# A decoder block on one core: the last output columns in two strided parts, gate rows by wide products, the state coefficients folded into C

## The reference, cut to what matters

```
mod = silu(c) @ w_ada + b_ada                      # six vectors of 1024: sh1 sc1 gt1 sh2 sc2 gt2
h = rms_norm(x, g_mix) * (1 + sc1) + sh1
u, q, k, v, ga, gb = split(h @ w_in)
# branch A: complex diagonal state space, 32 groups of 16 channels, 64 states each
bbar = coef * b                                    # coef, b complex, coef per (group, state)
state[t] = abar * state[t-1] + bbar @ u[t]
y = Re(c_re + i c_im applied to state) + d * u
y_a = glu(gelu(y) @ w_glu)
y_b = attention(rotary(q), rotary(k), v) @ w_attn_o
x = x + gt1 * ((sigmoid(ga) * y_a + sigmoid(gb) * y_b) @ w_out)
h2 = rms_norm(x, g_ffn) * (1 + sc2) + sh2
x = x + gt2 * experts(h2)                          # router, top 4 of 32, each expert:
        # gate_up = h2 @ w_gu[e] (1024 by 2048), clamped SwiGLU, @ w_down[e] (1024 by 1024)
out = rms_norm(x, g_final)
```

## Time and profile before

| what | value |
| --- | --- |
| median of three runs | 1161.6 us (1161.04 to 1162.45) |
| the profiled execution's own time | 1159.92 us |
| its span | 1158.0 us |
| TensorE busy | 1122.6 us (97%) |
| VectorE busy | 442.8 us (38%) |
| ScalarE busy | 140.9 us (12%) |
| GpSimd busy | 105.1 us (9%) |
| moved by DMA | 459.46 MB, mean 397 GB/s |
| chain that ended last | TensorE 78%, DMA 18% |

### The profile page before, as it was taken

How to read it: one execution, slowest core, us unless ns; L and a number is a source line. 1 busy time by engine, 2 the same in 40 slices (tenths; PEclk the granted TensorE clock), 3 DMA queues, 4 the chain that set the end, 5 groups by cost and what they waited for, 6 DMA issues and landing times.

```text
span 1158.0 us, 17087 instructions
## 1 busy us (share of the span) xinstructions
PE 1122.6 (97%) x6970; PEld 491.0 (42%) x6970; DVE 442.8 (38%) x952; ACT 140.9 (12%) x313; POOL 105.1 (9%) x142
## 2 busy tenths in 40 slices
PE   8999999999999999999999999999999999999996
PEld 6657788544333333333333333333333333333332
DVE  7857668263222333332222322222222222222224
ACT  3222240231000000000000000000000000000002
POOL 6496810000000000000000000000000000000000
PEclk9999999999999999999999999999999999999999
DMA  9983389999999999999999999999999999999994
GB/s 385 393 305 102 101 335 400 421 349 422 423 427 434 428 428 430 431 430 430 430 434 429 429 432 430 431 425 431 431 430 431 430 431 432 431 431 426 427 424 202
DMA packets 39839, 459.46 MB, mean 397 GB/s; under 512 B 3732, under 2 KB 4248, under 8 KB 16120
## 3 DMA queue, kind: packets, MB, share of 16 engines
q1 hardware_dynamic: 39088, 458.09, 94.3%
q10 hardware_dynamic: 712, 0.81, 0.2%
HBM read 457.83 MB, written 1.05 MB: 396 GB/s over the span
## 4 chain that ended last, share of the span: by engine, by line
PE 78%; DMA 18%; DVE 1%; ACT 1%; issue 1%; SPq 1%; DVEq 0%
PE ps L1086 30%; PE ps L1133 17%; DMA ring<-in_w_gu 16%; PE ps L662 5%; PE ps L1054 4%; PE ps L998 3%; PE ps L847 2%; PE ps L659 2%; PE ps L1110 2%; PE ps L865 2%; DMA ring<-in_first 1%; PE ps L830 1%; PE ps L922 1%; PE ps L623 1%; PE ps L629 1%; PE ps L1118 1%
## 5 line engine op out<-in xcount | busy, mean ns | idle before, releaser
L1086 PE MATMUL ps<-ring,zone 128*64 128x512 f32 x1024 | 227.0, 595 | 9.6 <-DMA ring<-in_w_gu 9.6
L1133 PE MATMUL ps<-ring,tmp 128*64 128x512 f32 x1012 | 224.2, 594 | 10.4 <-ACT tmp L1363 10.4
L1086 PE MATMUL ps<-zone 128*64 128x512 f32 x1024 | 227.2, 595 | 1.3 <-DMA zone<-in_w_gu 1.2
L1854 DVE TENSOR_TENSOR x_tok<-x_tok,ps 128x512 f32<-128x512 f32 x128 | 81.9, 681 | 261.4 <-PE ps L1054 260.1
L1086 PEld LDWEIGHTS ps<-ring,zone 128*64 128x64 f32 x1024 | 70.7, 137 | 161.6 <-issue 143.5
L1133 PEld LDWEIGHTS ps<-ring,tmp 128*64 128x64 f32 x1012 | 83.2, 137 | 130.7 <-issue 130.7
L1086 PEld LDWEIGHTS ps<-zone 128*64 128x64 f32 x1024 | 70.7, 137 | 154.1 <-issue 146.9
L1360 ACT ACTIVATE tmp<-hT 128x256 f32<-128x256 f32 x64 | 23.9, 417 | 722.8 <-DVE hT L1869 722.8
L1869 DVE TENSOR_SCALAR hT<-ps 128x256 f32<-128x256 f32 x64 | 24.2, 419 | 189.9 <-PE ps L1086 189.9
L1848 DVE TENSOR_TENSOR tmp<-ps,zone 128x512 f32<-128x512 f32 x32 | 22.1, 691 | 162.8 <-PE ps L1133 162.8
L1054 PE MATMUL ps<-tmp,xn_tok 64*128 64x512 f32 x248 | 70.0, 641 | 0.0
(11 more groups left out here) (339 smaller groups left out, 889.5 us busy)
## 6 DMA issues: line engine op xcount, KB each, us to landing
ring<-in_w_down SPq DMA_DIRECT2D x60, 2048.0 KB, 17.8
zone<-in_w_gu SPq DMA_DIRECT2D x23, 4096.0 KB, 26.9
ring<-in_w_gu SPq DMA_DIRECT2D x23, 4096.0 KB, 29.2
zone<-in_w_gu SPq DMA_DIRECT2D x14, 2048.0 KB, 13.1
ring<-in_w_gu SPq DMA_DIRECT2D x13, 2048.0 KB, 14.1
ring<-in_w_ada SPq DMA_DIRECT2D x16, 1024.0 KB, 13.1
ring<-in_w_in SPq DMA_DIRECT2D x12, 1024.0 KB, 14.6
ring<-in_w_gu SPq DMA_DIRECT2D x10, 1024.0 KB, 9.5
```

The source lines that it names most:

```text
L1086: last = mm(ps[CAP * h:CAP * h + CAP, b, :], hg[:, 2 * j + kk, :], w[:, kk, D * b + 512 * h:D * b + 512 * h + 512], start=False, stop=(j = ...
L1133: last = mm(ps[CAP * h:CAP * h + CAP, 3, :], actT[:, q, j, :], row[:, 512 * h:512 * h + 512], start=False, stop=(j == DN_PIECES - 1 and q ...
L1854: V.tensor_tensor(x_tok[:, t, 512 * h:512 * h + 512], x_tok[:, t, 512 * h:512 * h + 512], ps[:, bank + h, :], ALU.add).then_inc(S["comb_ad ...
```

## The change

1. B comes from the host in block form (`b_layout`, 512 KB in place of 256 KB) and goes straight into `BT`. The six weighting operations of VectorE, ScalarE's spreading, `b_columns` and the copy of its result are gone. In their place VectorE runs `weighted_c` on C: six operations of 512 elements a row, all with both inputs in SBUF, between the signal `phases` and `recurrence(0)`. ScalarE's negation of C (L1264) is gone.
2. `b_u(0)` and `b_u(1)` are one call, pair 1 into banks 6 and 7.
3. `modulation_products` makes two products in place of four, and its transposes have 64 rows. The gates are made directly on all rows by `gate_products` (two products of 512 columns for each n), to which VectorE adds the biases. These come with a new transfer, `gate_laid` (768 KB), behind `xs_read`. `gate_row` and ScalarE's two copies are gone.
4. The last 512 output columns of the second tokens are made in two parts of 256: of each four columns, two. Part 1 goes into bank 7, part 2 into bank 6, which waits for `x1` at 2, since the first half's result lies there. The pieces' `w_used` rises in part 2. Adding, squaring, transposing and routing of the last columns are cut accordingly; one `fill` is gone.

```diff
-    return np.concatenate([b[0].reshape(ST, 2, N, C).transpose(1, 2, 0, 3).reshape(P, ST * C) for b in (b_re, b_im)], axis=1)
+    out = np.zeros((4, 2, C, 2, KW, 2, N), np.float32)
...
+    def by_two(ap):
+        return ap.rearrange("p (n b) -> p n b", b=2)
+    def two_of_four(ap, g):
+        return ap.rearrange("p (n b) -> p n b", b=RUN)[:, :, 2 * g:2 * g + 2]
...
-            sp.dma_start(b_in.rearrange("p r s c -> p (r s c)"), b_laid[:, :]).then_inc(S["const_in"], 16)
+            sp.dma_start(BT.rearrange("p r m n -> p (r m n)"), b_laid[:, :]).then_inc(S["const_in"], 16)
...
             sp.wait_ge(S["xs_read"], KW)
+            sp.dma_start(gates[:, 0:D + W], gate_laid[:, :]).then_inc(S["gates_in"], 16)
             half_gu(0, 1, 0), half_gu(0, 1, 1)
...
             proj(2, 0)
-            b_columns()
             turned_columns(0)
             proj(2, 1, (0,))
-            b_u(0)
+            b_u(0, 1)
             proj(2, 1, (1, 2, 3))
             proj(3, 0)
-            b_u(1)
             turned_columns(1)
...
+                if n == 1:
+                    pe.wait_ge(S["row_sb"], 1)
                 pe.wait_ge(S["ada_used"], KD * n)
                 pe.wait_ge(S["ones_set"], 1)
-                for j in range(4):
-                    last = mm(ps[32 * j:32 * j + 32, MOD_BANK[n], :], ones[:, 0:32], ada_sum[n][:, 512 * j:512 * j + 512],
+                for j in range(2):
+                    own = 512 * (2 * (2 - n) + j)
+                    last = mm(ps[32 * j:32 * j + 32, MOD_BANK[n], :], ones[:, 0:32], ada_sum[n][:, own:own + 512],
...
+            def gate_products(n):
+                pe.wait_ge(S["ada_used"], KD * n)
+                pe.wait_ge(S["ones_set"], 1)
+                for h in range(2):
+                    if n == 1:
+                        last = mm(ps[:, 6 + h, :], ones[:, :], ada_sum[1][:, 512 * h:512 * h + 512], start=True, stop=True, skip_group_check=True)
+                    else:
+                        last = mm(ps[CAP * h:CAP * h + CAP, 7, :], ones[:, 0:CAP], ada_sum[2][:, D + 512 * h:D + 512 * h + 512],
+                                  start=True, stop=True, skip_group_check=True)
                 last.then_inc(S["row_up"], 1)
...
-            for h in range(2):
+            for part, bank in enumerate((6, 7, 6)):
+                if part == 1:
+                    pe.wait_ge(S["row_sb"], 2)
+                if part == 2:
+                    pe.wait_ge(S["x1"], 2)
                 for n in range(4):
...
-                        last = mm(ps[:, 6 + h, :], mergedT[:, k, P:T], w[:, kk, 512 * h:512 * h + 512],
-                                  start=(k == 0), stop=(k == KD - 1))
-                    if h == 1:
+                        if part == 0:
+                            last = mm(ps[:, bank, :], mergedT[:, k, P:T], w[:, kk, 0:W], start=(k == 0), stop=(k == KD - 1))
+                        else:
+                            last = mm(by_two(ps[:, bank, 0:T]), mergedT[:, k, P:T], two_of_four(w[:, kk, W:D], part - 1),
+                                      start=(k == 0), stop=(k == KD - 1))
+                    if part == 2:
                         last.then_inc(w_used, 1)
...
+            def weighted_c():
+                cr, ci = (sprm[:, j, :].unsqueeze(2).to_broadcast([P, ST, 2 * C]) for j in (3, 4))
+                c0, c1 = (CT[:, r].rearrange("p m (s c) -> p (m s) c", s=4) for r in range(2))
+                t0, t1 = (tmp[:, r, :].rearrange("p (s c) -> p s c", s=ST) for r in range(2))
+                link(V.tensor_tensor(t0, c1, ci, ALU.mult))
+                link(V.tensor_tensor(t1, c0, ci, ALU.mult))
+                link(V.tensor_tensor(c0, c0, cr, ALU.mult))
+                link(V.tensor_tensor(c1, c1, cr, ALU.mult))
+                V.tensor_tensor(c0, c0, t0, ALU.subtract).then_inc(S["c_set"], 1)
+                V.scalar_tensor_tensor(c1, t1, -1.0, c1, ALU.mult, ALU.subtract).then_inc(S["c_set"], 1)
+                dve.wait_ge(S["c_set"], 2)
...
             V.engine_nop().then_inc(S["phases"], 1)
+            weighted_c()
...
-            ada_part(8)
+            dve.wait_ge(S["gates_in"], 16)
+            dve.wait_ge(S["row_up"], 1)
+            V.tensor_tensor(gate_mix, ps[:, 6:8, :].rearrange("p b n -> p (b n)"), gate_mix, ALU.add).then_inc(S["row_sb"], 1)
+            ada_part(8), ada_part(9)
             modulation(1)
...
+            def add_two_of_four(g, bank):
+                scr = by_two(xn_tok[:, 1, W + T * g:W + T * g + T])
+                own = two_of_four(x_tok[:, 1, W:D], g)
+                link(V.tensor_tensor(scr, by_two(bank), two_of_four(gate_mix[:, W:D], g), ALU.mult))
+                V.tensor_tensor(own, own, scr, ALU.add).then_inc(S["x1"], 1)
```

More of the change, by code:

```diff
@@ L112, in b_layout, with gate_layout @@
 def b_layout(b_re, b_im):
-    return np.concatenate([b[0].reshape(ST, 2, N, C).transpose(1, 2, 0, 3).reshape(P, ST * C) for b in (b_re, b_im)], axis=1)
+    out = np.zeros((4, 2, C, 2, KW, 2, N), np.float32)
+    for r, w in enumerate((b_re, b_im)):
+        w = w[0].reshape(KW, 4, 2, N, C)
+        for q in range(2):
+            out[:, q, :, r, :, q, :] = w[:, :, q].transpose(1, 3, 0, 2)
+    return out.reshape(P, 2 * KW * P)
+def gate_layout(b_ada):
+    out = np.zeros((P, D + W), np.float32)
+    out[:, 0:D] = b_ada[0, 2 * D:3 * D]
+    for h in range(2):
+        out[CAP * h:CAP * h + CAP, D:] = b_ada[0, 5 * D + W * h:5 * D + W * h + W]
+    return out
 def c_layout(c_re, c_im):
@@ L127, in build @@
 def build(nc, x, w_ada, w_in, w_glu, w_attn_o, w_out, w_router, b_router, w_gu, b_gu, w_down, b_down, g_final,
-          const, head_in, first_in, pair_in, b_laid, c_laid, out):
+          const, head_in, first_in, pair_in, b_laid, c_laid, gate_laid, out):
     ctx = ExitStack()
@@ L665, in proj, with b_u @@
                     last.then_inc(w_used, 1)
-            def b_u(j):
-                if j == 0:
+            def b_u(*pairs):
+                if pairs[0] == 0:
                     pe.wait_ge(S["proj_sb"], 1)
-                    pe.wait_ge(S["BT_sb"], 1)
+                    pe.wait_ge(S["const_in"], 48)
                 else:
-                    pe.wait_ge(S["scanned"], 4 * j)
+                    pe.wait_ge(S["scanned"], 4 * pairs[0])
                 for r in range(2):
[L675 to L680, removed]
+                    for j in pairs:
+                        for q in range(2):
+                            s = 2 * j + q
+                            a = 32 * (s % 4)
+                            last = mm(ps[:, BU_BANK[j] + q, T * r:T * r + T], BT[a:a + 32, r, s // 4, :], uT[a:a + 32, s // 4, :],
+                                      start=True, stop=True, skip_group_check=True)
+                last.then_inc(S["bu_up"], len(pairs))
             def c_x(m):
@@ L806, in modulation_columns @@
                 for cb in range(4):
-                    last = nc.tensor.transpose(ps[:, MOD_BANK[n], P * cb:P * cb + P], modrow.rearrange("p (n b) -> p b n", b=RUN)[:, cb, :], ident)
+                    last = nc.tensor.transpose(ps[:, MOD_BANK[n], CAP * cb:CAP * cb + CAP],
+                                               modrow[0:CAP].rearrange("p (n b) -> p b n", b=RUN)[:, cb, :], ident[0:CAP, 0:CAP])
                 last.then_inc(S["modT_up"], 1)
[L810 to L817, removed]
+            def gate_products(n):
+                pe.wait_ge(S["ada_used"], KD * n)
+                pe.wait_ge(S["ones_set"], 1)
+                for h in range(2):
+                    if n == 1:
+                        last = mm(ps[:, 6 + h, :], ones[:, :], ada_sum[1][:, 512 * h:512 * h + 512], start=True, stop=True, skip_group_check=True)
+                    else:
+                        last = mm(ps[CAP * h:CAP * h + CAP, 7, :], ones[:, 0:CAP], ada_sum[2][:, D + 512 * h:D + 512 * h + 512],
+                                  start=True, stop=True, skip_group_check=True)
                 last.then_inc(S["row_up"], 1)
@@ L915, in _ @@
                     modulation_products(2)
+                    gate_products(2)
                     router_shift()
@@ L1137, in _ @@
             item(0, 0, 1, first=True, odd=32)
-            gate_row(1)
             item_table()
```

114 lines of the change are left out of this document (44 added, 70 removed).

## The result

| | median of the runs | runs |
| --- | --- | --- |
| kernel before | 1160.61 us (1159.24 to 1162.45) | 10 |
| changed kernel | 1164.57 us (1163.61 to 1166.07) | 10 |
| ratio | 1.0036, 95% interval 1.0029 to 1.0044 | |

The change makes the kernel 4.0 us slower. The forecast, 1163.8 us, lies 0.8 us from the measured time and its range holds it. Part of that closeness is luck. The forecast difference was +2.2 us and the measured one is +4.0, so the sum of the steps was too small by 1.8 us. The starting point hid 1.0 us of it: the forecast was laid on the median of three runs, 1161.6 us, and these three belong to the ten above, whose median is 1160.61. By the edge that the prediction set itself, 2.3 us, the change is slower, to which it gave a chance of 0.39; the larger chance, 0.49, went to no change. The experiments have to say which steps were too small.

The account below looks back on a forecast made before the run. DMA bounds the kernel: the end follows the moment it starts running without a gap. Later slots (+0.9) and the later output stage (+1.3) gave +2.2 us, laid on the 1161.6 median: 1163.8 us, range 1159.3 to 1166.8.

Parts of the forecast that it names:

- What bounds the kernel: Whole span: the end is when DMA starts running without a gap, plus 380 MB at 428 GB/s, plus an unchanged tail.
- B's blocks and the joint call: TensorE before turned_columns(1): dropped transposes save 0.9 us, the joint b_u 1.06, making it due at 73.5 instead of 75.47.
- weighted_c meets GpSimd: VectorE before recurrence(0): five of six operations slow to 1.52 us, 8.3 us in all, ending at 66.3 instead of 62.3.
- turned_columns(1) at 76.1: TensorE waits for VectorE's rotary(1), which ends at 76.1 instead of 75.47: 0.6 us late, bounds -1.2 and +2.0.
- Gates and modulation: Glu and output stages: products exchanged, -0.1 us in the first and +0.8 in the second.
- c_x and GpSimd delay nothing: GpSimd's 2.3 us delay meets TensorE at c_x(0), 17 us on; costed at nothing, under 1 us if uncovered.
- The last columns in two parts: Output stage's end: w_out's first slot frees 3.3 us later, second dip vanishes, gapless DMA starts at 254.9, not 254.0: +0.9.
- The meeting free: VectorE before recurrence(0): meeting GpSimd costs nothing, TensorE is 1.9 us early, end -0.3, 1161.3 us; chance 0.22.
- The first item decides: DMA near 252 us: the first expert item's release, not w_out's slots, starts the gapless run; 1158.9 us; chance 0.12.
- Half rate: Last columns: strided instructions take 0.43 us each, 6.9 us a part, slots 3.9 us further back; 1167.7 us; chance 0.11.
- the shift of the stage: Output stage runs later by 0.6 - 0.1 + 0.8 = 1.3 us, from the late turned_columns(1) and changed products.

Follow-up runs that it names:

- e6_late_slots: Kernel before plus one SyncE wait, holding four transfers until the last of w_out's slots is free; 1163.58 us, +3.15 (1.0025).
- e11_no_split: Changed kernel without the last columns in two strided parts; 1162.51 us, +2.0 against the kernel before (1.0021).
- e3_split: Kernel before with only the last columns in two strided parts; 1161.19 us, +0.8 (1.0005).
- state part: Kernel before with only B's blocks from the host, weighted_c on C beside GpSimd and the joint b_u; 1162.73 and 1162.84 us, +2.4 each.
- e12_filled: Kernel before with B's blocks, weighted_c, joint b_u, plus four unneeded products before TensorE's wait for rotary(1); 1162.02 us, +1.2 (1.0006).
- e1_state: Kernel before with only B's blocks from the host, weighted_c on C beside GpSimd and the joint b_u; 1162.73 us, +2.4 (1.0020).
- e1b_state_again: Second run of the kernel before with only host B blocks, weighted_c beside GpSimd and the joint b_u; 1162.84 us, +2.4 (1.0016).
- e5_state_early: Kernel before with only host B blocks, joint b_u and weighted_c, moved ahead of rotary(0) where GpSimd is idle; 1158.40 us, -2.0 (0.9983).
- e4_early: Changed kernel with weighted_c moved ahead of rotary(0), where GpSimd is idle; 1161.99 us, +1.6 against the kernel before (1.0013).
- e8_signal_behind: Changed kernel with the signal that starts GpSimd's tables moved behind weighted_c; 1165.80 us, +5.4 against the kernel before (1.0055).

## Why the prediction was right, point by point

- *What bounds the kernel.* Right, and now shown rather than read. `e6_late_slots` moves nothing but the moment of DMA's last gap, and the end follows (+3.15 us). That the bytes behind the gap give the end holds only to 1 or 2 us, as `e11_no_split` and `e3_split` show.
- *B's blocks and the joint call.* Right. 16 instructions of b_u took 1.15 us where 8 took 1.13.
- *weighted_c meets GpSimd.* Right in mechanism and size. Predicted 0.7 and five of 1.52; the profile after has one of 0.69 and five of 1.41 to 1.63, and recurrence(0) at 66.87 (predicted 66.3, before 62.31):

```profile
58.69 0.69 DVE L1556 TENSOR_TENSOR tmp<-zone,sprm 128x512 f32<-128x512 f32 x1
59.41 1.41 DVE L1557 TENSOR_TENSOR tmp<-zone,sprm 128x512 f32<-128x512 f32 x1
...
62.31 1.63 DVE L1559 TENSOR_TENSOR zone<-zone,sprm 128x512 f32<-128x512 f32 x1
...
66.87 0.69 DVE L1597 TENSOR_TENSOR tmp<-ps,zone 128x512 f32<-128x512 f32 x1
```

- *turned_columns(1) at 76.1.* It came at 76.43, held by the rotary as said:

```profile
76.43 1.06 PE L718 MATMUL ps<-head,zone 128*128 128x128 f32 x8 [2.09 <-DVE zone L1575]
```

  Of its 0.96 us against 75.47, 0.7 stem from a wait for an early transfer near 20 us (0.97 us in this execution, none in that of before). Eleven of the fourteen profiles have such a wait, of 0.26 to 1.28 us, also `e3_split` and `e6_late_slots`, which alter nothing that early, so it isn't the change's. Hence the step's own delay is 0.2 to 0.3, not 0.6. **The first step that failed is the price of this wait**: I priced the pause by what it delays and not by what the clock does behind it. That term, 1.7 us in the executions that have it, stood in no line of the sum. The state part was forecast at +0.6 and measured +2.4 twice, and `e12_filled` takes about half of it back. The clock accounts for about 1 us of the miss. The other 0.8 us are there in runs of full clock too, and the idle time at 176 us below may be part of them.
- *Gates and modulation.* **The second step that failed**, by its size. The glu stage, from its first new product (176.46, before 175.00) to the output stage (207.88, before 205.98), grew by 0.44 us where -0.1 was predicted (the four terms that the prediction names add up to -0.4, or to -0.2 against the start-to-start times of 0.99 and 1.78 us, so the miss is larger than it looks); the output stage, to the second tokens' start (225.60, before 222.25), by 1.45 where +0.8 was. Two terms were wrong. Two products of `modulation_products` take as long as the four before, 4 instructions 1.05 us against 8 in 1.07, as if those four, each with 32 columns of its own, had run side by side. And transposes of 64 rows are not shorter: 0.69 us for four against 0.63. The new products were nearly as sized, 1.96 and 1.08. The 16 instructions of the output projection beside them took 0.2 us longer than before (3.63 us from start to start in place of 3.53, twice), for a cause that no run tests:

```profile
214.84 1.05 PE L804 MATMUL ps<-hT,ones 128*32 128x512 f32 x4
215.82 1.08 PE L824 MATMUL ps<-hT,ones 128*64 128x512 f32 x4
...
221.02 0.69 PE L812 MATMUL ps<-head,zone 64*128 64x64 f32 x4
```

- *A step that was missed.* In the profile after TensorE stands idle for 0.62 us ahead of 176.46, where it had no pause before. ScalarE's last sigmoid of the gates ends at 172.21 us in place of 170.73, later than the shift of the stage, behind a longer issue of its own transfers. The profiles of `e1_state`, `e1b_state_again` and `e5_state_early` show 0.62 to 0.83 us there, those of `e4_early` and `e12_filled` nothing, and `e3_split` and `e6_late_slots`, which alter nothing ahead of it, 0.2. It counts for 0.5 us in the profile after; its cause was not tested, and how much of it is the change's stays open.
- *c_x and GpSimd delay nothing.* Right: c_x(0) has no wait in the profile after. The cover was real but thin, as `e8_signal_behind` shows.
- *The last columns in two parts.* The mechanism is right to the view: slots late, first dip deeper, second gone. The price predicted was +0.9; it measured +0.8 alone, 1.7 to 2 with the rest. The strided rate was predicted at 3.45 us a part and came at 3.89 (3.72 dense). The Trainium skill's rule (SBUF — State Buffer, section Door 1: The DMA port swizzle), by which two hits in a line of 16 bytes keep the full rate, is met to within these 5%.
- *Rivals.* The meeting free: refuted by the operations' times. The first item decides: refuted by `e6_late_slots`. Half rate: refuted by 3.89 us.

In numbers, by the profile: the shift of the stage, forecast at 1.3, came to 2.6 us (0.2 at turned_columns(1), 0.5 at 176 us, 0.4 and 1.45 in the two stages); with 0.9 for the slots that is 3.5. A slow clock in some executions adds 0.4: the six of the ten runs with a mean clock of 0.998 have a median of 1164.15 us, all ten 1164.57. By the experiments: state part +2.4 (forecast 0.6), gates +1.3 (0.7), two parts +0.8 (0.9), +4.5 in all. The two accounts agree roughly on the total and on the slots, but not on how much of the rest is the state part and how much the gates. In the changed kernel, moving `weighted_c` brought 2.6 us, and the traces show as much without any clock: TensorE is 2.2 us earlier at turned_columns(1) (74.20 against 76.43) and 2.7 at the first gate product (173.72 against 176.46), since the idle time at 176 us is gone too. Whether the clock falls less often in the changed kernel (4 low means of 10) than in the state part alone (14 of 23) can't be told from so few runs.

## What to carry to other kernels

Follow the moment from which the bottleneck queue runs without a gap; the bytes still to come behind the last gap give the end in one line of the DMA view, here to within 2 us and no better. A pause of TensorE of two microseconds is not priced by its length: a fall of the granted clock may come behind it, in some executions and not in others, so one clean profile doesn't clear it. A median that exceeds its own profile by 2 us with a wide spread is the sign, and the mean clock of each timed run, where it is on record, is the next thing to read. When folding work from one engine into a gap of another, look for a gap in which the third is idle too: with the same six operations the state part was worth -2.0 us in the idle stretch that ends at 50 us and +2.4 us at 59.

## What the runs showed that was not expected

- The clock behind a pause: two stretches at 0.58 and 0.57 after 2.08 us of idle TensorE, a like fall after 2.09 us in `e11_no_split`, full clock after 2.08 or 2.09 us in three other executions, and full clock after 2.66 us (`e8_signal_behind`).
- Without any such pause (none over 1.2 us in the 30 us before), the last down piece took 8.72 to 8.78 us in place of 7.09 in the profiles of three kernels, at a clock of 0.92 and 0.74 in the changed kernel's. What starts it stays open.
- Four float32 products with 32 columns of output each cost as much as two: 1.07 and 1.05 us.
